# RWKV scan: order of PSUM banks for 64x64 products, and two 128-column steps turned into 64x64 products

## The chip, the cores and the metric

One core of one Trainium2 chip runs the whole program. The time is device microseconds of one execution, as the median of several runs; lower is better. All data are float32. TensorE is called PE below, VectorE DVE, ScalarE ACT, GpSimd POOL and SyncE SP.

## The reference, cut to what matters

The program is one step of a two-layer trunk: an attention and HGRN2 layer, an RWKV-7 layer, an MLP behind each. The change is in the RWKV-7 layer alone. Its mixer runs, for 16 heads of size 64, forward and backward over 512 sample tokens and 128 prompt tokens, this recurrence:

```
def step(s, inp):
    r_t, w_t, k_t, v_t, kk_t, a_t = inp
    sa = jnp.einsum('bhvk,bhk->bhv', s, -kk_t)
    s = s * w_t[:, :, None, :] + sa[..., None] * (kk_t * a_t)[:, :, None, :] + v_t[..., None] * k_t[:, :, None, :]
    return s, jnp.einsum('bhvk,bhk->bhv', s, r_t)
...
kk = kk * lax.rsqrt(jnp.maximum(jnp.sum(kk * kk, axis=-1, keepdims=True), 1e-24))
...
mu = jnp.mean(y, axis=-1, keepdims=True)
var = jnp.mean(jnp.square(y - mu), axis=-1, keepdims=True)
```

The sums over the 64 elements of a head (of kk squared, of y, of y centred and squared, and of the bonus r k) are the "head sums" below.

## The kernel before, in words

The kernel does the recurrence in chunks of 64 tokens. Inside a chunk the products of the states' updates are a triangular matrix that is inverted by repeated squaring; from chunk to chunk a 64x64 state is carried. The work is laid out in 40 iterations: 8 pairs of heads (q) by 5 tiles of 128 tokens (two chunks), each iteration for both heads of the pair and both directions. Each task of an iteration m is a set of 8, 16 or 24 small products; d is the direction, h the head, hh the chunk. HALF[0] and HALF[1] are the partitions 0 to 63 and 64 to 127. A product whose operands lie in HALF[a] and whose output lies in HALF[b] uses one quarter (a, b) of PE's array, called a tile of the array here; a product with 64 rows and 128 output columns uses a half of it, as does one of 128 rows and 64 columns. A float32 product makes two matmul records and two weight loads in the trace; a transpose makes one of each.

The order of the work on each engine is written out by hand: PE_ORDER, DVE_ORDER, ACT_ORDER and POOL_ORDER list the tasks of an iteration, and each engine goes through its list 46 times (n from -4 to 41), skipping what does not apply. Engines wait for each other by semaphores. PE's list is:

```
PE_ORDER = ("gate", "values", "k_sum", "mean", "B4", ("G", 2), ("s1", -1), ("final", -1), "B5", ("GR", 1), "x0", ("B1", 1), ("A1", 2), "u0",
            "a", "bonus", "state", "prompt", "s0", ("B2", 1), "w", ("A2", 2), "x1", ("B3", 1), ("BT", 1), "u1", ("A3", 2), ("var", 1))
```

(in the first iteration of a pair w stands behind x1 and BT behind A3). A number is how many iterations ahead the task works. What the names mean:

- G, A1, A2, A3 (gram, squares, fourths, eighths): 16, 16, 24 and 16 products of 64x64 on all four tiles, for the inverse.
- B1 (diagonal), B2 (off_diagonal, 16 products each on four tiles, into banks 2 and 3), then B3, B4, B5 (first_block, second_block, third_block): three times on_token, 8 products of 64x64 each. Their operands and outputs lie in the same half, so they use two of the four tiles, and all of them write bank 2, columns 0 to 255. B3 waits for ACT's copy of bank 2 (NT, line 2383). DVE adds each result to DD (block, line 2505).
- GR (read_keys, line 2198): 8 products with 64 rows, 128 output columns and 128 moving columns, into banks 6 and 7; DVE masks them into KB (line 2494, two instructions).
- BT (turn_keys, line 2238): 8 transposes of the same keys, 64 rows and 128 columns, into banks 6 and 7; ACT copies them out (line 2393).
- The walk over the two chunks of an iteration: x (x0, x1: 4 products; DVE adds XV, line 2515), u (4 products of the states with the queries into banks 4 and 5, 4 of TTs with XS; ACT copies out, line 2399), s (8 products with 128 rows and 64 columns; DVE updates the states, line 2526). ACT line 2408 copies y out.
- Work on the side that uses banks 6 and 7 as GR and BT do, each behind the other's copy-out (`before`, evacuated): the head sums (head_sums, line 2079) for k_sum, mean, var and bonus; lora (prompt, w, a; line 2087: four tiles, 128 or 512 moving columns), values (five transposes, line 2132), gate (wide), state, final.

Nearly all products are issued through the helper `mm` at line 178, so the trace gives that line to them; the transposes of BT (2238) and of values (2132) have their own. ACT copies bank 3 of B2 into XV at line 2387, right after NT at line 2383. In the last iterations products of the next stage (out1, 128x128) stand between the tasks of the list ("ahead").

Of the kernel before, what the change touches and what calls it, by code (L numbers as in the profile page):

```python
# [17 lines left out]
ALU = mybir.AluOpType  # L18
# [85 lines left out]
HN = T // 2  # L104
# [11 lines left out]
def program(nc, a, o):  # L116
    with ExitStack() as ctx:
# [1951 lines left out]
        def rwkv_pe(pe):  # L2069
# [6 lines left out]
            def head_sums(rhs):  # L2076

                for b, (t0, n) in enumerate(GROUPS):
                    for h, r in enumerate(HALF):
                        ins = mm(PS[r, 6 + b, 0:n], CON[r, C_BD64 + 64 * h:C_BD64 + 64 * h + 64], rhs[r, t0:t0 + n])  # L2080
                return ins
# [65 lines left out]
            def on_token(bank, lhsT, rhs):  # L2147

                for hh, h, d in ALL8:
                    c0 = 128 * h + 64 * hh  # L2150
                    ins = mm(PS[HALF[d], bank, c0:c0 + 64], lhsT[HALF[d], h, hh, :], rhs[HALF[d], h, hh, :])
                return ins
# [39 lines left out]
            def read_keys(m):  # L2192
                if before[0]:
                    evacuated(pe, before[0])
                before[0] = ("GR", m)
                pe.wait_ge(S("rwkv_staged"), m + 1)
                for hh, d, h, c in units_of(m):
                    ins = mm(PS[:, 6 + h, 256 * d + 128 * hh:256 * d + 128 * hh + 128], BKD[d][HALF[h], c, :], ARD[d][HALF[h], c, :])
                ins.then_inc(S("b_product"), 1)
# [21 lines left out]
            def first_block(m):  # L2221
                pe.wait_ge(S("b_scalar"), 4 * m + B_SC["N"])
                on_token(2, NT[:, :, 0], DD[:, :, 0]).then_inc(S("b_product"), 1)
# [9 lines left out]
            def turn_keys(m):  # L2233
                if before[0]:
                    evacuated(pe, before[0])
                before[0] = ("BT", m)
                for hh, d, h, c in units_of(m):
                    ins = nc.tensor.transpose(PS[:, 6 + h, 128 * d + 64 * hh:128 * d + 64 * hh + 64], BKD[d][HALF[h], c, :],
                                              CON[HALF[h], C_ID + 64 * h:C_ID + 64 * h + 64])
                ins.then_inc(S("b_product"), 1)  # L2240
# [23 lines left out]
            def walk_u(n, s):  # L2264
                q, k = n // 5, 2 * n + s
                pe.wait_ge(S("rwkv_x"), k + 1)
                for d, h, hh, c in each_dh(n, s):
                    mm(PS[HALF[h], 4 + d, 192 + 64 * hh:256 + 64 * hh], ST[d][HALF[h], c, :], ARD[d][HALF[h], place(q, c), 64:128],
                       start=False, stop=False, shared=True)
                for d, h, hh, c in each_dh(n, s):  # L2270
                    ins = mm(PS[HALF[d], 4 + h, 64:128], TTs[n % 2][HALF[d], h, 0, hh, :], XS[HALF[d], h, :], start=False, stop=True, shared=True)
                ins.then_inc(S("rwkv_u_psum"), 1)
# [24 lines left out]
        def rwkv_act(act, step):  # L2297
# [7 lines left out]
            def side(item):  # L2305
# [34 lines left out]
                elif kind == "bonus":  # L2340
                    act.wait_ge(S("rwkv_bonus_psum"), q + 1)
                    A.activation(BN[q % 2], pair(6), ACT.Copy, scale=64.0).then_inc(S("rwkv_bonus"), 1)
                elif kind == "var":
                    log_exp()
                    act.wait_ge(S("rwkv_var"), q + 1)
                    step(A.activation(RT2, pair(6), ACT.Ln, bias=EPSC[:, 1:2]))
# [82 lines left out]
        def rwkv_dve(dve, step):  # L2429
# [14 lines left out]
            def k_max(q):  # L2444
                dve.wait_ge(S("rwkv_k_sum"), q + 1)
                V.tensor_scalar(RT, pair(6), 1e-24 / 64, None, ALU.max).then_inc(S("rwkv_k_max"), 1)
# [56 lines left out]
            def block(m, what, out):  # L2503
                dve.wait_ge(S("b_product"), 8 * m + B_PR[what])
                V.tensor_tensor(out[:, :, 0], PS[:, 2, 0:256].rearrange("p (h c x) -> p h c x", h=2, c=2), DD[:, :, 0], ALU.add).then_inc(S("b_vector"), 1)  # L2505
# [24 lines left out]
            def side(item):  # L2530
# [3 lines left out]
                elif kind == "mean":  # L2534
                    dve.wait_ge(S("rwkv_mean"), q + 1)
                    V.tensor_tensor(K[:, q, :], YS, pair(6), ALU.subtract).then_inc(S("rwkv_centred"), 1)
# [480 lines left out]
```

## Time and profile before

| | |
|---|---|
| three runs | 2218.49, 2219.36, 2223.67 us; median 2219.36 us |
| span of the profiled execution (the only time known of it) | 2224.3 us |
| PE busy | 2055.9 us, 92% of the span, 26203 records |
| DVE, ACT, POOL busy | 64%, 47%, 14% |
| RWKV scan | about 1190 to 1725 us of the span |
| one pair of heads in the scan's steady part | 65 us (five iterations of 13.0 us) |

Busy time on PE is counted from a record's start to its modelled end. Records overlap, since a product of 64 columns takes 218 ns but starts a few ns behind its neighbour on another tile of the array; so the rows give starts and lengths of pieces, and the rate at which products go has to be taken from these.

### The profile page before, as it was taken

The page shows a single profiled execution, that of the slowest core. Times are in us where ns is not written, and L with a number is a line of the kernel's source. Part 1 is how long each engine was busy: PE and PEld are TensorE (multiplying, and loading weights), DVE is VectorE, ACT ScalarE, POOL GpSimd, SP SyncE. Part 2 cuts the span into 40 slices and gives each one's busy share as a digit, 9 for nine tenths or more (in the row PEclk, how much of TensorE's full clock was granted, in tenths as well). Part 3 has the DMA queues.
Part 4 walks back from the last instruction along what each step waited for, and adds up shares of the span by engine and source line. Part 5 has one row for each costly group of instructions (what it writes and reads, how often), then busy time and mean ns, then how long its engine had stood idle before and what let it go on. Part 6 is the DMA issues. An engine that isn't in the chain of part 4 may idle for free.

```text
span 2224.3 us, 60454 instructions
## 1 busy us (share of the span) xinstructions
PE 2055.9 (92%) x26203; PEld 1837.2 (83%) x26203; DVE 1414.5 (64%) x2698; ACT 1042.6 (47%) x1887; POOL 312.1 (14%) x542
## 2 busy tenths in 40 slices
PE   5999877898999999989997888898888989999999
PEld 2789754478999999957996777777777989999999
DVE  2242475655667675877535888887784468585857
ACT  5242363434535353565334665665654254434353
POOL 1000131101000000010002444444342200000000
PEclk8999999999999999999998999999999999999999
DMA  8212206960231322113210000000000221322212
GB/s 286 78 39 79 79 1 235 353 216 20 76 95 58 102 70 95 57 36 107 80 39 8 8 10 7 8 10 10 10 21 28 78 76 57 95 68 85 94 59 86
DMA packets 129764, 167.86 MB, mean 75 GB/s; under 512 B 13900, under 2 KB 87388, under 8 KB 129372
## 3 DMA queue, kind: packets, MB, share of 16 engines
q1 hardware_dynamic: 129500, 164.00, 22.0%
q8 instruction: 208, 3.41, 0.6%
q14 instruction: 56, 0.46, 0.1%
HBM read 160.44 MB, written 3.54 MB: 74 GB/s over the span
## 4 chain that ended last, share of the span: by engine, by line
PE 69%; DVE 14%; issue 7%; ACT 7%; POOL 1%; DMA 1%; PEld 1%; PEldq 0%; POOLq 0%; DVEq 0%; SPq 0%; ACTq 0%
PE psum L178 68%; DVE arena L2494 2%; ACT arena L1857 1%; ACT arena L1411 1%; DVE arena L2441 1%; DVE arena L2526 1%; DVE arena L2473 1%; DVE arena L2472 1%; PEld psum L178 1%; DVE arena L2465 1%; DVE arena L2505 1%; DVE small L1377 1%; DMA arena<-in_x_prompt 0%; DVE arena L2474 0%; PE psum L1342 0%
## 5 line engine op out<-in xcount | busy, mean ns | idle before, releaser
L178 PE MATMUL psum<-arena 64*64 64x64 f32 (+4 forms) x16064 | 582.3, 239 | 97.5 <-ACT arena L1411 14.9
L178 PEld LDWEIGHTS psum<-arena 64*64 64x64 f32 (+3 forms) x16064 | 462.5, 140 | 227.2 <-issue 109.4
L178 PE MATMUL psum<-hidden_high,weights_high 128*128 128x320 f32 x896 | 277.1, 309 | 0.5 <-DVE arena L1020 0.5
L178 PE MATMUL psum<-hidden_low,weights_high 128*128 128x320 f32 x896 | 276.9, 309 | 0.0
L178 PE MATMUL psum<-hidden_high,weights_low 128*128 128x320 f32 x896 | 276.9, 309 | 0.0
L178 PE MATMUL psum<-norm_high,weights_high 128*128 128x320 f32 x960 | 218.8, 309 | 0.0
L178 PE MATMUL psum<-norm_high,weights_low 128*128 128x320 f32 x960 | 218.7, 309 | 0.0
L178 PE MATMUL psum<-norm_low,weights_high 128*128 128x320 f32 x960 | 218.7, 309 | 0.0
L178 PEld LDWEIGHTS psum<-hidden_high,weights_high 128*128 128x128 f32 x896 | 168.2, 188 | 0.9 <-issue 0.7
L178 PEld LDWEIGHTS psum<-hidden_low,weights_high 128*128 128x128 f32 x896 | 168.2, 188 | 0.0
L178 PEld LDWEIGHTS psum<-hidden_high,weights_low 128*128 128x128 f32 x896 | 168.2, 188 | 0.0
L178 PEld LDWEIGHTS psum<-norm_low,weights_high 128*128 128x128 f32 x960 | 160.6, 188 | 0.0
L178 PEld LDWEIGHTS psum<-norm_high,weights_high 128*128 128x128 f32 x960 | 160.5, 188 | 0.0
L178 PEld LDWEIGHTS psum<-norm_high,weights_low 128*128 128x128 f32 x960 | 160.5, 188 | 0.0
L999 DVE TENSOR_TENSOR hidden<-hidden 128x640 f32<-128x640 f32 x32 | 26.4, 826 | 175.6 <-ACT hidden L946 175.6
L944 ACT ACTIVATE hidden<-psum 128x640 f32<-128x640 f32 x64 | 45.1, 705 | 189.4 <-PE psum L178 189.4
L899 ACT ACTIVATE weights_high<-weight_sums 128x512 fp32r<-128x512 f32 x128 | 76.8, 624 | 106.6 <-DVE weight_sums L918 55.7
L621 POOL TENSOR_TENSOR arena<-arena 128x640 f32<-128x640 f32 x24 | 41.7, 1739 | 570.7 <-ACT arena L613 569.9
L2610 POOL TENSOR_TENSOR arena<-arena,constants 64x128 f32<-64x128 f32 x160 | 79.1, 494 | 172.4 <-DVE arena L2485 157.8
L1020 DVE SCALAR_TENSOR_TENSOR arena<-psum,ada,arena 128x128 f32<-128x128 f32 (+2 forms) x208 | 83.7, 432 | 30.0 <-PE psum L178 29.1
L903 DVE TENSOR_TENSOR weights_low<-weight_sums,weights_high 128x512 fp32r<-128x512 f32 x128 | 88.5, 702 | 8.4 <-ACT weights_high L899 8.4
L899 ACT ACTIVATE weights_high<-weights 128x512 fp32r<-128x512 f32 x96 | 58.2, 622 | 68.2 <-PE psum L178 68.2
(268 smaller groups left out, 3985.6 us busy)
## 6 DMA issues: line engine op xcount, KB each, us to landing
weights<-in_mlp_w SPq DMA_DIRECT2D x64, 1024.0 KB, 5.4
arena<-in_ada_w SPq DMA_DIRECT2D x24, 2048.0 KB, 9.5
arena<-in_ab_w_in SPq DMA_DIRECT2D x6, 2048.0 KB, 7.9
arena<-in_ab_w_out SPq DMA_DIRECT2D x2, 2048.0 KB, 9.2
arena<-in_rwkv_wv SPq DMA_DIRECT2D x2, 2048.0 KB, 8.2
arena<-in_rwkv_wr SPq DMA_DIRECT2D x2, 2048.0 KB, 8.2
arena<-in_rwkv_wk SPq DMA_DIRECT2D x2, 2048.0 KB, 7.8
arena<-in_x_sample SPq DMA_DIRECT2D x1, 2048.0 KB, 10.0
```

The lines of the kernel that those rows point to most:

```text
L178: return nc.tensor.matmul(out, lhsT, rhs, start=start, stop=stop, skip_group_check=shared)
L621: G.tensor_tensor(total, a0 if k == 1 else total, (a0, a1)[k % 2], ALU.add).then_inc(S("norm_squares_added"), 1)
L899: A.activation(slots_of(WHI)[:, j], slot_raw(l, grp, i, j), ACT.Copy).then_inc(S("slot_high"), 1)
L903: V.tensor_tensor(slots_of(WLO)[:, j], slot_raw(l, grp, i, j), slots_of(WHI)[:, j], ALU.subtract)\
L944: A.activation(h, PS[:, 2 * j:2 * j + 2, 0:HN], ACT.Relu).then_inc(S("up_evacuated"), 1)
L999: V.tensor_tensor(h[:, H_T1:H_T3 + 1, :], h[:, H_B11:H_B22 + 1:3, :], h[:, H_B12:H_B12 + 1, :].broadcast_to([P, 2, HN]), ALU.subtract)\
L1020: ins = V.scalar_tensor_tensor(x, PS[:, bank, c:c + t1 - t0], gate[:, m, g:g + 1], x, ALU.mult, ALU.add)
L1377: step(V.tensor_reduce(st[:, 0:1], pair(2 * h, k), AXX, ALU.max))
L1411: A.activation(PR[m % 2][:, h, 0:k], pair(2 * h, k), ACT.Exp, scale=ATTN_SCALE, bias=st[:, 1:2], accum_out=st[:, 2:3]).then_inc(S("att_exp ...
L1857: A.activation(XI[s % 2][:, k, :], unit(U_H, 8)[:, k, :], ACT.Identity, scale=OMM[:, 8 * mrow + k:8 * mrow + k + 1])\
L2494: ins = V.tensor_tensor(KB[m % 2][:, h], PS[:, 6 + h, :].rearrange("p (d w x) -> p d w x", d=2, w=2), both.unsqueeze(2).broadcast_to([P, 2 ...
L2610: ins = G.tensor_tensor(P1[HALF[h], d, 0], QD[r, h, 0], units(r), ALU.add)
```

## The change

- on_token (B3, B4, B5): the order of the loops alternates the heads between the directions, and head h writes bank 2 + h, columns 256 to 383, in place of all in bank 2, columns 0 to 255. DVE's block reads from there. B3 waits for ACT's copy XV of bank 3 (line 2387) in place of NT of bank 2 (line 2383), because it now writes into bank 3.
- head_sums: two groups of 320 tokens in place of 512 and 128, in an order in which the halves write different banks. The four readers take two times 320 elements from two banks.
- read_keys (GR): 16 products of 64x64 with 128 moving columns, in place of 8 with 128 output columns.
- turn_keys (BT): 16 products of 64x64 with a 64x64 identity, in place of 8 transposes.
- walk_u (u): the same 8 products in another order, so that neighbours lie on different tiles of the array and in different banks.

```
             def head_sums(rhs):
 
-                for b, (t0, n) in enumerate(GROUPS):
-                    for h, r in enumerate(HALF):
-                        ins = mm(PS[r, 6 + b, 0:n], CON[r, C_BD64 + 64 * h:C_BD64 + 64 * h + 64], rhs[r, t0:t0 + n])
+                for h, g in ((0, 0), (1, 1), (0, 1), (1, 0)):
+                    r = HALF[h]
+                    ins = mm(PS[r, 6 + g, 0:HN], CON[r, C_BD64 + 64 * h:C_BD64 + 64 * h + 64], rhs[r, HN * g:HN * g + HN])
                 return ins
...
             def on_token(bank, lhsT, rhs):
 
-                for hh, h, d in ALL8:
-                    c0 = 128 * h + 64 * hh
-                    ins = mm(PS[HALF[d], bank, c0:c0 + 64], lhsT[HALF[d], h, hh, :], rhs[HALF[d], h, hh, :])
+                for h0 in range(2):
+                    for hh in range(2):
+                        for d in range(2):
+                            h = h0 ^ d
+                            c0 = 256 + 64 * hh
+                            ins = mm(PS[HALF[d], bank + h, c0:c0 + 64], lhsT[HALF[d], h, hh, :], rhs[HALF[d], h, hh, :])
                 return ins
...
                 for hh, d, h, c in units_of(m):
-                    ins = mm(PS[:, 6 + h, 256 * d + 128 * hh:256 * d + 128 * hh + 128], BKD[d][HALF[h], c, :], ARD[d][HALF[h], c, :])
+                    for r in HALF:
+                        ins = mm(PS[r, 6 + h, 256 * d + 128 * hh:256 * d + 128 * hh + 128], BKD[d][HALF[h], c, r], ARD[d][HALF[h], c, :])
                 ins.then_inc(S("b_product"), 1)
...
             def first_block(m):
-                pe.wait_ge(S("b_scalar"), 4 * m + B_SC["N"])
+                pe.wait_ge(S("b_scalar"), 4 * m + B_SC["XV"])
                 on_token(2, NT[:, :, 0], DD[:, :, 0]).then_inc(S("b_product"), 1)
...
                 for hh, d, h, c in units_of(m):
-                    ins = nc.tensor.transpose(PS[:, 6 + h, 128 * d + 64 * hh:128 * d + 64 * hh + 64], BKD[d][HALF[h], c, :],
-                                              CON[HALF[h], C_ID + 64 * h:C_ID + 64 * h + 64])
+                    for r in HALF:
+                        ins = mm(PS[r, 6 + h, 128 * d + 64 * hh:128 * d + 64 * hh + 64], BKD[d][HALF[h], c, r],
+                                 CON[HALF[h], C_ID + 64 * h:C_ID + 64 * h + 64])
                 ins.then_inc(S("b_product"), 1)
...
                 pe.wait_ge(S("rwkv_x"), k + 1)
-                for d, h, hh, c in each_dh(n, s):
+                at = {(d, h): (d, h, hh, c) for d, h, hh, c in each_dh(n, s)}
+                for d, h, hh, c in (at[0, 0], at[1, 1], at[1, 0], at[0, 1]):
                     mm(PS[HALF[h], 4 + d, 192 + 64 * hh:256 + 64 * hh], ST[d][HALF[h], c, :], ARD[d][HALF[h], place(q, c), 64:128],
                        start=False, stop=False, shared=True)
-                for d, h, hh, c in each_dh(n, s):
+                for d, h, hh, c in (at[0, 1], at[1, 0], at[0, 0], at[1, 1]):
                     ins = mm(PS[HALF[d], 4 + h, 64:128], TTs[n % 2][HALF[d], h, 0, hh, :], XS[HALF[d], h, :], start=False, stop=True, shared=True)
                 ins.then_inc(S("rwkv_u_psum"), 1)
...
-                    A.activation(BN[q % 2], pair(6), ACT.Copy, scale=64.0).then_inc(S("rwkv_bonus"), 1)
+                    A.activation(in_halves(BN[q % 2]), halves(6), ACT.Copy, scale=64.0).then_inc(S("rwkv_bonus"), 1)
...
-                    step(A.activation(RT2, pair(6), ACT.Ln, bias=EPSC[:, 1:2]))
+                    step(A.activation(in_halves(RT2), halves(6), ACT.Ln, bias=EPSC[:, 1:2]))
...
-                V.tensor_scalar(RT, pair(6), 1e-24 / 64, None, ALU.max).then_inc(S("rwkv_k_max"), 1)
+                V.tensor_scalar(in_halves(RT), halves(6), 1e-24 / 64, None, ALU.max).then_inc(S("rwkv_k_max"), 1)
...
-                V.tensor_tensor(out[:, :, 0], PS[:, 2, 0:256].rearrange("p (h c x) -> p h c x", h=2, c=2), DD[:, :, 0], ALU.add).then_inc(S("b_vector"), 1)
+                V.tensor_tensor(out[:, :, 0], PS[:, 2:4, 256:384].rearrange("p h (c x) -> p h c x", c=2), DD[:, :, 0], ALU.add).then_inc(S("b_vector"), 1)
...
-                    V.tensor_tensor(K[:, q, :], YS, pair(6), ALU.subtract).then_inc(S("rwkv_centred"), 1)
+                    V.tensor_tensor(in_halves(K[:, q, :]), in_halves(YS), halves(6), ALU.subtract).then_inc(S("rwkv_centred"), 1)
```

`halves(6)` is columns 0 to 319 of banks 6 and 7; `in_halves(x)` is x as two groups of 320.

## Rows read from the trace of the kernel before

**Rows 1.** The page's busy line: us, share of the span, records.

```profile
PE 2055.9 (92%) x26203; PEld 1837.2 (83%) x26203; DVE 1414.5 (64%) x2698; ACT 1042.6 (47%) x1887; POOL 312.1 (14%) x542
```

**Rows 2.** Busy us (records) in stretches, one pair of heads each; then clock, DMA.

```profile
1311.00:1376.00 65.00, 58.17 (x1893) 48.14 (x1894) 53.41 (x118) 39.88 (x96) 28.78 (x60) 1.00 0.04 9
```

**Rows 3.** Waits in the scan's steady part, 1220 to 1680: us, times, longest.

```profile
DVE arena L2515 <- PE psum L178: 27.1, 29, 2.2
...
PE psum L178 <- issue: 4.6, 8, 1.0
```

**Rows 4.** The chain that ended last, 1190 to 1735: start us, us, what.

```profile
1196.22 4.21 PE psum L178 x80
...
1255.75 0.39 PE psum L2238 x8
1256.15 1.12 PE psum L178 x43
...
1311.03 3.56 PE psum L178 x96
...
1698.21 5.22 PE psum L178 x100
...
1709.83 0.39 PE psum L2238 x8
...
1719.67 2.87 PE psum L178 x40
```

**Rows 5.** PE in order of time: B5's last records, then GR, then x0.

```profile
1312.79 0.40 PE L178 MATMUL psum<-arena 64*64 64x64 f32 x8
...
1313.12 1.16 PE L178 MATMUL psum<-arena 64*128 64x128 f32 x15
...
1314.21 0.34 PE L178 MATMUL psum<-arena 64*64 64x64 f32 x7
```

**Rows 6.** PE in order of time, pieces of one kind of product.

```profile
1310.28 0.68 PE L178 MATMUL psum<-arena 64*64 64x64 f32 x16 [0.37 <-DVE arena L2505]
...
1340.37 0.67 PE L178 MATMUL psum<-arena 64*64 64x128 f32 x16 [0.46 <-DVE arena L2494]
...
1366.61 0.73 PE L178 MATMUL psum<-arena 64*64 64x64 f32 x16
```

**Rows 7.** PE in order of time: B5 to u0 in one piece.

```profile
1312.55 3.43 PE L178 MATMUL psum<-arena 64*64 64x64 f32 x120
```

**Rows 8.** PE in order of time: x1 and B3, BT, u1 and A3.

```profile
1319.88 0.81 PE L178 MATMUL psum<-arena 64*64 64x64 f32 x24 [0.48 <-DVE arena L2526]
1320.62 0.46 PE L2238 MATMUL psum<-constants,arena 64*128 64x64 f32 x8
1321.01 1.20 PE L178 MATMUL psum<-arena 64*64 64x64 f32 x48
```

**Rows 9.** DVE in order of time, the XS add of x0 in two iterations.

```profile
1314.62 0.29 DVE L2515 TENSOR_TENSOR arena<-psum,arena 128x128 f32<-128x128 f32 x1 [0.89 <-PE psum L178]
...
1353.11 0.29 DVE L2515 TENSOR_TENSOR arena<-psum,arena 128x128 f32<-128x128 f32 x1
```

**Rows 10.** DVE in order of time: the add after A3.

```profile
1322.24 0.42 DVE L2500 TENSOR_TENSOR arena<-psum,constants 128x256 f32<-128x256 f32 x1 [1.09 <-PE psum L178]
```

**Rows 11.** Late in the scan: an x0 behind GR, ACT's XV copy, the next BT.

```profile
1641.90 0.52 PE L178 MATMUL psum<-arena 64*64 64x64 f32 x18 [0.21 <-ACT arena L2408]
...
1684.70 0.38 ACT L2387 ACTIVATE arena<-psum 128x256 f32<-128x256 f32 x1
...
1685.63 0.46 PE L2238 MATMUL psum<-constants,arena 64*128 64x64 f32 x8
```

**Rows 12.** First iteration of a pair, in order of time: head sum, B4, B4's reader.

```profile
1347.37 1.29 PE L178 MATMUL psum<-arena,constants 64*64 64x512 f32 x8 [0.69 <-ACT arena L2393]
1348.50 0.63 PE L178 MATMUL psum<-arena 64*64 64x64 f32 x16
...
1349.86 0.42 DVE L2505 TENSOR_TENSOR arena<-psum,arena 128x256 f32<-128x256 f32 x1
```

## The prediction

> **What bounds the kernel now.** I read the page first [rows 1]: PE is busy 92% of the span. The change touches only the RWKV scan, so I cut that out in stretches of one pair of heads [rows 2]: of 65 us PE is busy 58.2 and DVE 53.4, with a granted clock of 1.00, the 2.4 GHz level. Neither is alone the bound: DVE's XS add, the one after x, waits for PE 27.1 us in 460 [rows 3], and the chain below goes over both. Both go through fixed lists and hold each other up, so a saving on PE counts only where the chain that ended last runs over PE. So I took that chain piece by piece and held against it every GR, BT and u [rows 4]. On it lie 14 of the scan's 40 GR (the first in the piece at 1196.22, the last in that at 1698.21), 12 of 40 BT (1255.75 to 1709.83) and 23 of 80 u (the first in the piece at 1256.15, the last in that at 1719.67). In the steady part these are, of five iterations, one GR (n mod 5 = 3, the piece of 3.56 us at 1311.03), one BT in that same iteration and two or three u. The rest of the chain is DVE's and ACT's.
>
> **The change part by part.** A record's own length stands in every piece: 0.22 us for 64 moving columns, 0.27 for 128. The last record starts that much before the piece's end.
>
> *The rate of products.* B4, 16 records on two tiles of the array, takes 0.68 us (the row at 1310.28 in [rows 6]): 0.68 - 0.22 = 0.46 us from first start to last. x1 and B3 together, 24 records, take 0.81 [rows 8]: 0.59 from first to last. Both come out with a step of 0.058 us for each group (one record on each tile in use), 0.05 once where PE begins again, and up to 0.02 inside a group: 0.05 + 7 x 0.058 = 0.46, and 0.05 + 2 x 0.058 + 7 x 0.058 + 0.02 = 0.59. With 128 moving columns lora shows four tiles at once (1340.37 in [rows 6]): 16 records in 0.67, so (0.67 - 0.27 - 0.05 - 0.02) / 3 = 0.11 per group of four.
>
> *GR* [rows 5]. B5 ends at 1313.19, so its last record started at 1312.97, and GR starts at 1313.12: 0.15 where 0.058 is usual, 0.09 too much. GR itself is 1.16 - 0.27 = 0.89 from first to last start. The last starts at 1314.01, x0 at 1314.21: 0.20 where the step is 0.11, 0.09 too much; then 0.05 for beginning again. After the change there are 32 records in 8 groups of four, at lora's step 7 x 0.11 + 0.02 = 0.79 in place of 0.89, with no change of shape on either side. Saved: 0.09 + 0.10 + 0.09 + 0.05 = 0.33 us, and 0.02 for the stagger inside the last group, 0.35 at most; I take 0.34. The piece B5 to u0 checks it [rows 7]: 120 records, 3.43 - 0.22 = 3.21 from first to last. B5, x0, B1, A1 and u0 are 8 + 2 + 8 + 8 + 7 = 33 steps, 1.91; u0's own loss 0.05; that leaves 1.25 for GR with both changes of shape, less the 0.90 of its 8 steps: 0.35.
>
> *BT* [rows 8]. B3's last record starts at 1320.69 - 0.22 = 1320.47, BT at 1320.62 (0.15), its last 0.24 later, u1 another 0.15 later, and 0.05 for beginning again: 0.59. New: 8 groups of four at 0.058 = 0.47 in place of 0.24, and one step of 0.058 to follow: 0.53. Saved 0.06 where u1 follows at once. But its result comes later: 0.49 after B3's last start, not 0.39. ACT's copy of it and the next side task stand behind that. In the first iteration of a pair BT stands behind A3, with no array change to save in front of it that is not covered by a wait, and the next head sum waited 0.69 us for ACT's copy [rows 12]; there the head sum and B4 come up to 0.24 later. B4's reader on DVE starts at 1349.86, and B4's results were there at about 1348.50 + 0.63 = 1349.13. So 0.24 is covered by 0.7 us; without that cover it would cost 0.24 x 8 = 1.9 us.
>
> *u* (1366.61 in [rows 6]). The same 16 records on the same two tiles as B4, but 0.73 in place of 0.68: its second four go tile A, A, B, B. In the new order they alternate: saved 0.05.
>
> *Bank order of on_token and head_sums.* B4 writes all to one bank from two halves, and still goes at one pair per 0.058, the step at which four-tile work goes too; the two tiles are full. Value 0. From below: nothing to gain under the step of a full tile. From above: nothing, as x0 writes two banks at the same step. A head sum is 8 records in 1.29 us [rows 12], two halves side by side. Its stream per half is 640 columns twice, before and after; the sum over 512 and 128 is that over 320 and 320. Value 0, within 0.05 each way; the readers have the same 640 elements.
>
> *The Trainium skill speaks against splitting into more products.* Its page "TensorE: Matmul & The Clock Gate" (Part 1, the section on 56 against 53.3 ns) says starts are never closer than about 25 ns. By that figure BT's 32 records would last 0.8 us, an estimate, and 12 x 0.33 = 4 us of the gain would be gone. The trace says otherwise for just this kind of product on four tiles: B1 and A1, 64 records, fit into 3.21 us with all the rest only at 0.058 us for four, 15 ns each [rows 7], so the rule gets no chance here.
>
> *B3's new wait.* XV's copy ends 0.28 us after NT's. In most iterations x1's wait stands between. In the last of a pair it doesn't: late in the scan XV ends at 1684.70 + 0.38 = 1685.08 [rows 11], while B3, whose last record starts 0.15 before BT at 1685.63, began at 1685.02. B3 will be 0.06 late and a hop of some 0.05 more: 0.1 to 0.15. Behind it stand BT, u1 and A3. Three such lie on the chain (near 1461, 1592 and 1685): 3 x 0.15 = 0.45 us lost.
>
> *More instructions.* 16 records more for GR and 24 for BT, on 379 per iteration (1893 / 5): 11%. PE's idle time put to "issue" is 4.6 us, 8 times [rows 3]. If it grows with the count, 0.5 us, at most all on the chain; at least 0. I take 0.3.
>
> *Sum.* GR: twice in the last iterations (1640, 1679) x0 waited for ACT's y copy behind GR (1641.90 in [rows 11]), so half counts: 12 x 0.34 + 2 x 0.17 = 4.4. BT: 12 x 0.06 = 0.7. u: 23 x 0.05 = 1.15. Together 6.3; less 0.45 and 0.3: 5.5 us. This is also close to the most that can come of it, since the old chain stays a lower bound for the new time. Is there room beside it? At x0 of the steady part DVE sat idle 0.89 (1314.62 in [rows 9]), more than the 0.34; at A3, after BT and u1, 1.09 [rows 10], more than 0.11. Where GR isn't on the chain DVE comes to x0 straight from other work, with no idle time before it (1353.11 in [rows 9]), and nothing is won.
>
> The profiled execution has a span of 2224.3 us, 4.9 above the median and 0.6 above the slowest of the three runs. A difference of 5.5 us does not depend on that. Against the median 2219.4: **2213.9 us**, 0.25% faster. A measurement of this kernel can tell about 0.3% (6.7 us) from no change.
>
> **The rivals.**
>
> *A: the cover is thinner.* DVE, ACT and the walk are each busy or late right behind PE's chain; what PE gives, they take back. For it: DVE busy 53.4 of 65. Against it: the two idle times above. The tail's five GR have no such row, and if these 1.5 us, half of the u and the fill's three GR go, 5.5 - 1.5 - 0.6 - 1.0 = 2.4: 2217 us.
>
> *B: more than the chain shows.* PE's other GR, BT and u shorten too, 40 x (0.34 + 0.06) + 80 x 0.05 = 20 us in all. If the chain as inferred misses part of PE's share, say half of the rest, (20 - 6.3) / 2 = 7 more: 2207 us. For it: DVE waits for PE 27.1 us at x alone [rows 3]. Against: behind many of these waits ACT or DVE is next.
>
> *C: slower. Two products with the same rows and the same moving columns don't run side by side.* New GR and BT are all such pairs. Then GR goes at 0.11 per two records, 16 x 0.11 = 1.8 us, 0.9 more less 0.34 of saved changes; BT at 0.058 per two, 0.93, 0.46 more less 0.06. On the chain: 14 x 0.56 + 12 x 0.40 = 12.6, less 1.15 of u, plus 0.75: 12 us slower, 2231.6. It decides from a group step in GR of 0.15 up (0.04 x 8 x 14 = 4.5 us, the gain gone). Against it: lora's two column halves share rows and moving columns, and go at 0.11 per four.
>
> *D: BT's later result stalls the side tasks.* The 1.9 us above and as much again where ACT's copy stands before its u copy: gain 5.5 - 3.8 = 1.7, 2217.7. I count it with A.
>
> **How the numbers follow.** Forecast 0.58, A with D 0.22, B 0.14, C 0.06. The forecast's own range is 2212 to 2216 (terms of 0 to 0.6 each way, and 1 us for the medians). For 8 in 10 it reaches over all of A to 2218 and into B to 2209. Faster by over 0.3% needs 2212.7 or less: 0.35 of the forecast (0.20), B whole (0.14): 0.34. Slower: C, 0.05. Same: the rest, 0.61.
>
> **What would show it.** In the trace after: B5, GR, x0 and B1 in one piece without a change of shape, B5 to u0 in 3.04 us in place of 3.43 [rows 7]; BT a part of a 64x64 piece, B3 to A3 0.1 shorter where nothing waits; u alone 0.68. The step from 1311 to 1376 would be 64.4 to 64.6 us in place of 65, the rest of the gain in fill and tail. DVE's idle time before x0's add would fall from 0.89 to 0.55 at n mod 5 = 3 and nothing move in the other four. B4 and the head sums as long as before. The prediction is wrong if GR's 32 records take over 0.95 us from first to last, if the step per pair of heads falls by over 1 us, or if it doesn't fall.

## The result, and the profile after: slower, and PE runs out of instructions

| | before | after |
|---|---|---|
| median of 20 runs each, on the same chips | 2223.5 us (2218.5 to 2230.0) | 2229.8 us (2225.6 to 2238.2) |
| span of the profiled execution | 2224.3 us | 2225.5 us |
| ratio | 1 | 1.0031, 95% interval 1.0024 to 1.0039 |

The change costs 0.31%, 6.9 us, where 5.5 us of gain were forecast. The two profiled executions differ by only 1.2 us in their spans, though the scan alone is 9.4 us longer (the table below): before the scan the changed kernel's execution happens to be 9 us ahead. Most of that, 6.7 us by the 3700th matmul record (518.4 us before, 511.6 after, where the 1500th came at 280.3 and 279.5), arises in stages that the change doesn't touch. So the scan is compared below, and not the spans.

The page of the changed kernel has, below its head, PE's line: against [rows 1] PE is busy 6.1 us *less*, with 1600 matmul records and 1600 weight loads more (3200 / 40 = 80 PE instructions more per iteration).

```profile
span 2225.5 us, 63654 instructions
...
PE 2049.8 (92%) x27803; PEld 1839.1 (83%) x27803; DVE 1413.0 (63%) x2698; ACT 1041.5 (47%) x1887; POOL 311.8 (14%) x542
```

So the array was busy for less time. The local sums of the prediction can be read in PE's order of time in the changed kernel. First B5 to u0 [rows 7], then B3's end and BT (the piece of 27 records, with no change of shape on either side) and u1 and the first product of A3 behind it [rows 8], then a u that stands alone [rows 6]:

```profile
1437.76 3.19 PE L178 MATMUL psum<-arena 64*64 64x64 f32 x136
...
1324.57 0.68 PE L178 MATMUL psum<-constants,arena 64*64 64x64 f32 x27
1325.06 1.29 PE L178 MATMUL psum<-arena 64*64 64x64 f32 x48
...
1360.36 0.68 PE L178 MATMUL psum<-arena 64*64 64x64 f32 x16 [0.38 <-DVE arena L2521]
```

B5 to u0 went from 3.43 to 3.19 us (3.04 was forecast), u from 0.73 to 0.68, and u1 starts 0.03 us after BT's last record (1324.57 + 0.68 - 0.22 = 1325.03) and not 0.15. Of the 0.15 us missing in GR, the records' starts show where it is: B5's last starts at 1438.17 and GR's first at 1438.30, as late as when the shape changed there, and its second group comes 0.16 us later where I had 0.11; the other six steps are 0.11, and x0 follows 0.09 behind the last.

What cost the time is in PE's waits over the scan, 1195 to 1720 (engine, line, what it waited for: us in total, times, longest):

```profile
PE psum L178 <- issue: 18.6, 37, 2.0
PE psum L178 <- ACT arena L2405: 8.1, 17, 0.7
...
PE psum L178 <- DVE arena L2521: 5.5, 13, 0.8
...
DVE arena L2521 <- PE psum L178: 35.9, 38, 2.1
```

In [rows 3] "issue" was 4.6 us, 8 times, and it is no more than that in the kernel before over this wider stretch. It is now 18.6 us, 37 times, and the longest wait of PE; 21 of the 37 are of 0.3 us or more and make 15.4 of the 18.6 us. "Issue" says that nothing in the records released the instruction. DVE's XS add (L2515 before, L2521 now) waits for PE hardly longer than it did; over the same stretch 1195 to 1720 it was, in the kernel before:

```profile
DVE arena L2515 <- PE psum L178: 34.7, 38, 2.2
```

Here is one of PE's stops for "issue", PE in order of time:

```profile
1387.03 0.68 PE L178 MATMUL psum<-arena 128*64 128x64 f32 x15
1388.06 2.27 PE L178 MATMUL psum<-arena 128*64 128x64 f32 x102 [0.35 <-issue]
1390.12 0.27 PE L178 MATMUL psum<-constants,arena 64*64 64x64 f32 x1
...
1390.22 0.52 PE L178 MATMUL psum<-constants,arena 64*64 64x64 f32 x20
1392.17 0.39 PE L178 MATMUL psum<-constants,arena 64*64 64x64 f32 x10 [1.43 <-issue]
```

BT stops in its middle for 1.43 us, after 22 of its 32 records and at the end of a run of 127 records without a pause (the chain below has 125 of them). No operand can be missing there: it is one task with one wait ahead of it. And the stop lies on the chain that ended last:

```profile
1387.70 0.35 issue
1388.06 2.68 PE psum L178 x125
1390.74 1.43 issue
1392.17 1.86 PE psum L178 x58
```

The DMA view shows a queue of its own for instructions, q8, in packets of 16 KB. In the stretch from 1264 to 1272, where no other queue is at work, two of them can be seen in 40 slices of 0.2 us, at 1264.9 and 1268.9:

```profile
GB/s 0 0 0 0 82 0 0 0 0 0 0 0 0 0 0 0 0 0 0 0 0 0 0 0 82 0 0 0 0 0 0 0 0 0 0 0 0 0 0 0
...
q8 instruction: 2, 0.03, 1.8%
```

PE stops and goes on at 1267.70 and 1271.37, 2.8 and 2.4 us behind their starts:

```profile
1267.70 1.12 PE L178 MATMUL psum<-arena 64*64 64x64 f32 x31 [0.73 <-issue]
...
1271.37 2.63 PE L178 MATMUL psum<-arena 64*64 64x64 f32 x80 [0.33 <-issue]
```

The stop in BT ends 2.3 us after the start of the packet of 1389.88. So it is throughout: of the changed kernel's 21 stops of 0.3 us and more, 20 end 2.2 to 2.8 us after a 16 KB packet of q8 has started (the other, the longest, 3.0 us), and so do all five of the kernel before. Between two packets there are never less than 3.3 us, in either kernel; the median is 4.16 us before and 3.86 after. Over the stretch 1200 to 1700, first before, then after:

```profile
q8 instruction: 115, 1.88, 1.6%
```

```profile
q8 instruction: 124, 2.03, 1.7%
```

Where the stops fall in the list of work says the same, more sharply. Here are the three stretches between the four stops that end at 1388.06, 1392.17, 1399.69 and 1403.9 (records of PE and of PEld):

```profile
1388.06:1392.16 4.10, 2.68 (x127) 2.39 (x128) 2.74 (x9) 2.41 (x7) 1.04 (x2) 1.00 0.20 52
1392.17:1399.68 7.51, 6.94 (x253) 6.07 (x252) 5.61 (x13) 3.98 (x9) 2.75 (x7) 1.00 0.02 4
1399.69:1403.89 4.20, 3.22 (x127) 2.78 (x127) 0.87 (x3) 3.61 (x11) 1.53 (x4) 1.00 0.01 4
```

That is 255, 505 and 254 instructions: one, two and one times the contents of a packet, as worked out below. Of the 20 distances between neighbouring long stops of the changed kernel 18 are whole multiples of 252 to 256; the two others are those on either side of the stop at 1549.29. PE stops where one packet's instructions are used up, whatever task it is in. Where two stops stand one packet apart, as here, that packet's worth takes 3.5 to 4.2 us.

The Trainium skill ("Runtime: NRT & Kernel Launch", Instruction fetch mechanics) says that an engine's instructions come in blocks of 16 KiB, 256 instructions, from a DMA queue. The counts agree: 16022 matmul records and 16019 weight loads (their row stands under "Instructions alone" below) in 127 packets are 252 per packet. The same section of the Trainium skill says that the fetch is hidden because instructions are dispatched more slowly than blocks come in. That does not hold here. By this trace's numbers alone, 252 per 3.3 us is 76 per us at the very most, and 252 per 3.5 to 4.2 us is 60 to 72 per us where PE starves; the scan asks for 32041 / 518.9 = 62 per us in the mean, and for about 117 per us in BT (27 records and as many loads in 0.68 - 0.22 = 0.46 us, the row at 1324.57).

### The profile page after: what moved, and what is told of

Same layout as the page of the kernel before. It is cut to its first block, busy times and chain, and to the rows that moved or that the text cites. A ratio compares the mean times of both kernels' runs of the same rounds, so it can differ in the third digit from the quotient of the medians.

```text
span 2225.5 us, 63654 instructions
## 1 busy us (share of the span) xinstructions
PE 2049.8 (92%) x27803; PEld 1839.1 (83%) x27803; DVE 1413.0 (63%) x2698; ACT 1041.5 (47%) x1887; POOL 311.8 (14%) x542
## 4 chain that ended last, share of the span: by engine, by line
PE 71%; DVE 10%; issue 7%; ACT 7%; POOL 2%; DMA 1%; PEld 1%; PEldq 0%; POOLq 0%; DVEq 0%; SPq 0%; ACTq 0%
PE psum L178 70%; DVE arena L2500 1%; ACT arena L1857 1%; ACT arena L1411 1%; DVE arena L2471 1%; PEld psum L178 1%; DVE small L1377 1%; DMA arena<-in_x_prompt 0%; DVE arena L2447 0%; PE psum L1342 0%; DVE arena L2479 0%; ACT arena L642 0%; DVE arena L2478 0%; DVE arena L2532 0%; POOL arena L621 0%
## 5 line engine op out<-in xcount | busy, mean ns | idle before, releaser
L178 PE MATMUL psum<-arena 64*64 64x64 f32 (+5 forms) x16704 | 578.0, 241 | 104.3 <-ACT arena L1411 15.0
L899 ACT ACTIVATE weights_high<-weights 128x512 fp32r<-128x512 f32 x96 | 58.2, 622 | 68.3 <-PE psum L178 68.3
```

Source lines behind the costliest of these rows:

```text
L178: return nc.tensor.matmul(out, lhsT, rhs, start=start, stop=stop, skip_group_check=shared)
L899: A.activation(slots_of(WHI)[:, j], slot_raw(l, grp, i, j), ACT.Copy).then_inc(S("slot_high"), 1)
```

## The experiments

Theory S: PE runs out of instructions, since the change adds 80 per iteration and each stretch of small products on four tiles eats them faster than they are fetched. Theory L: BT's longer stream and later result hold up what stands behind. Theory B: the bank order, the head sums' groups or B3's new wait do it.

All kernels beside the one before; "scan" is from the first product of the walk's state updates to the last, "stops" is PE's idle time in it put to issue, both read from one profiled execution, and the packets are those of 1200 to 1700. The ratios are to the runs of the kernel before on the same chip. Two ratios differ for sure only where they are some 0.0015 apart. The profiled execution of e4_gr_bt_alone was its slowest, that of e3_old_gr its fastest.

| kernel | PE instr. per iteration | ratio, 95% | scan us | stops us (times) | packets |
|---|---|---|---|---|---|
| before | 0 | 1 | 509.4 | 4.6 (8) | 115 |
| e1_old_gr_bt | 0 | 0.9992, 0.9981 to 1.0003 | 509.4 | 5.7 (13) | 114 |
| e8_gr_and_u | +32 | 0.9993, 0.9984 to 1.0001 | 508.2 | 7.1 (18) | 119 |
| e2_old_bt | +32 | 0.9989, 0.9980 to 0.9998 | 507.0 | 6.5 (20) | 120 |
| e3_old_gr | +48 | 1.0045, 1.0032 to 1.0058 | 518.5 | 13.5 (21) | 119 |
| e4_gr_bt_alone | +80 | 1.0028, 1.0016 to 1.0040 | 514.7 | 14.5 (24) | 124 |
| e12_change_again | +80 | 1.0035, 1.0022 to 1.0048 | 517.5 | 15.4 (30) | 125 |
| e5_half_bt | +48 | 1.0017, 1.0008 to 1.0025 | 515.6 | 14.0 (30) | 120 |
| e6_half_both | +16 | 1.0003, 0.9993 to 1.0014 | 510.7 | 8.5 (18) | 116 |
| e7_late_bt | +36 | 1.0014, 1.0006 to 1.0023 | 516.1 | 9.5 (21) | 118 |
| e9_before_fewer | -112 | 0.9968, 0.9956 to 0.9981 | 503.6 | 1.0 (2) | 98 |
| e11_old_bt_fewer | -80 | 0.9955, 0.9941 to 0.9969 | 502.4 | 1.9 (7) | 103 |
| e10_after_fewer | -32 | 0.9975, 0.9965 to 0.9986 | 505.2 | 4.1 (10) | 110 |
| e13_before_padded | +80 | 1.0043, 1.0031 to 1.0056 | 521.8 | 11.8 (20) | 123 |
| e14_fewer_padded | -32 | 0.9976, 0.9963 to 0.9988 | 506.1 | 1.5 (2) | 109 |

### Which part does it

The changed kernel with GR, BT or both as before, and the kernel before with the new GR and BT alone:

```
 def turn_keys(m):                                   # e1, e2
-        for r in HALF:
-            ins = mm(PS[r, 6 + h, ...], BKD[d][HALF[h], c, r], CON[HALF[h], C_ID + 64 * h:...])
+        ins = nc.tensor.transpose(PS[:, 6 + h, ...], BKD[d][HALF[h], c, :], CON[HALF[h], C_ID + 64 * h:...])
 def read_keys(m):                                   # e1, e3
-        for r in HALF:
-            ins = mm(PS[r, 6 + h, ...], BKD[d][HALF[h], c, r], ARD[d][HALF[h], c, :])
+        ins = mm(PS[:, 6 + h, ...], BKD[d][HALF[h], c, :], ARD[d][HALF[h], c, :])
```

> The changed kernel with both GR and BT as before; the order of u, the banks of on_token and head_sums and B3's new wait stay. PE has the instruction count of the kernel before. Theory S (supply: PE runs out of instructions, because GR and BT as 64x64 products add 80 instructions per iteration): PE's idle time put to issue in the scan falls back from 18.6 us (37 times) to about 5 (8), and the time is 0 to 2 us under that of before. Rival W (wait and banks: B3's wait for XV, or the new banks and groups, cost the time): still 4 to 8 us slower than before. Rival R (GR's and BT's own records last longer than computed): as S in the time, but the issue idle time does not tell it apart; the next runs do.

> The changed kernel with BT as transposes as before; GR is 64x64. 32 instructions per iteration more than before. Theory S: issue idle 8 to 12 us, time within 3 us of before, since what GR saves by the two changes of shape (0.34 us on 14 of the chain) stands against part of the stalls. Rival W: as the changed kernel, 6 us slower. Rival R for BT: all of the loss is gone, 4 to 5 us faster than before.

> The changed kernel with GR as before; BT is 64x64. 48 instructions per iteration more than before. Theory S: issue idle 8 to 14 us, 3 to 7 us slower than before, since BT saves only 0.06 us on the chain at a time. Rival W: 6 to 10 us slower. Rival R for GR: 1 to 2 us faster.

> The kernel before with GR and BT as 64x64 products and nothing else of the change. 80 instructions per iteration more. Theory S: issue idle 15 to 20 us, 5 to 9 us slower than before, like the changed kernel plus what u's order gave. Rival W: 4 to 5 us faster than before.

Measured: 0.9992, 0.9989, 1.0045, 1.0028. With both as before the loss is gone; bank order, head sums, u and B3's wait together are worth nothing or 0.1%: theory B falls. The new BT does it. With it the kernel is slow whether GR is new (the change) or old; without it, new GR and all, it is at least as fast as before. PE's waits in the scan of e2_old_bt, the idle time that was 18.6 us:

```profile
PE psum L178 <- issue: 6.5, 20, 0.8
```

The sizes were less well forecast than the signs: by theory S e2_old_bt would have had 8 to 12 us of stops (6.5 measured), e4_gr_bt_alone 15 to 20 (14.5), and e3_old_gr would have been 3 to 7 us slower (10). e2_old_bt and e3_old_gr ask for the same mean number of instructions per us (30172 / 507.0 and 30827 / 518.5, both 59.5), with 6.5 and 13.5 us of stops: the mean alone doesn't set them, the place where the instructions are added counts too.

The change was also run once more, unaltered, with the other kernels on one chip; it came out as the first time, with 15.4 us of stops:

> The changed kernel again, beside these on the same chip, for a second profile. All theories: 5 to 8 us slower than before. Theory S: issue idle in the scan 12 to 22 us, but at other places than in the first profile, since the fetches' landings vary.

The last of this group has GR and u new, and banks, head sums and BT's transposes as before, on the kernel before:

```
# before, with the change's read_keys and walk_u; on_token, head_sums, their readers and turn_keys as before
```

> The kernel before with GR as 64x64 products and the new order of u, nothing else: no new banks, no new wait for XV, no new groups of the head sums. Theory S: as the changed kernel with BT as transposes or better by the 0.5 us that B3's wait was computed at: 2 to 4 us faster than before, issue idle 5 to 9 us. If the banks matter (they let neighbours write side by side), it is slower than that kernel by over 2 us.

0.9993 beside the 0.9989 of e2_old_bt: the bank order and B3's wait are nothing that can be told.

### Number of instructions, or BT's place and length?

Half of the new BT, and half of BT and GR, in the same places with steps of the same length:

```
-                    for r in HALF:
+                    for r in HALF[0:1]:            # e5: in turn_keys; e6: in read_keys too
```

> The changed kernel, with BT made of only the 8 products whose output lies in partitions 0 to 63 (the other half of the turned keys is left out, and the copy-out multiplies by zero). These 8 go one behind the other on two tiles, so BT's stream lasts as long as that of the 16 on four tiles (8 steps of 0.058 us), without a change of shape, and its result comes as late; but 32 instructions per iteration are gone. Theory S (supply of instructions): most of BT's loss goes: issue idle in the scan from 18.6 us to 6 to 10, and the time 0 to 4 us under that of before. Rival L (BT's stream is longer and its result later, 0.1 to 0.2 us, and that costs the time): no change against the changed kernel, 5 to 7 us slower than before.

> As the run with half of BT, and GR too is made of only its 8 products for partitions 0 to 63 (the masks are zero, so the masked keys are). GR's stream stays 8 steps of 0.11 us. Against the changed kernel 64 instructions per iteration are gone; against the kernel before there are 16 more. Theory S: issue idle 4 to 7 us and 3 to 6 us faster than before, the gain that was predicted for the chain. Rival L: as the changed kernel, 5 to 7 us slower than before.

1.0017 and 1.0003: less with each step, as theory S has it, and BT's stream is as long as in the change. But neither theory's numbers were met: e5_half_bt is 3.8 us slower than before (theory S: 0 to 4 faster; theory L: 5 to 7 slower), e6_half_both 0.7 slower (theory S: 3 to 6 faster), and in e5_half_bt the stops had hardly fallen (14.0 us), with 32 instructions fewer. So I made BT late with few instructions, by a 64x128 product between its transposes:

```
                 for hh, d, h, c in units_of(m):
+                    if (hh, d, h) == (1, 1, 0):
+                        mm(PS[:, 7, 256:384], BKD[d][HALF[1], c, :], ARD[d][HALF[1], c, :])
                     ins = nc.tensor.transpose(...)
```

> The changed kernel with BT as transposes, and one product more in it (64 rows, 128 output and 128 moving columns, into unused columns of bank 7) before the last two transposes: BT's stream and its result are some 0.2 us later at a price of 4 instructions. Theory S: within 3 us of the same kernel without that product, which was 2.5 us faster than before; where BT is on the chain 12 x 0.2 = 2.4 us are lost, so 1 to 3 us faster to 1 slower than before. Rival L: 8 to 12 us slower than that kernel, 6 to 10 slower than before.

1.0014, 3.1 us slower than before and 0.25% above e2_old_bt: a longer BT costs as well. Theory S had it at most 1 us slower than before, theory L 6 to 10 us slower; neither was met, and the stops rose too (9.5 us for 6.5). But the product makes the whole stream 0.28 us longer, u1 and A3 start that much later, and five iterations take 65.5 us where e2_old_bt takes 64.65. In the change BT with u1 is *shorter*: the row at 1325.06 above. The run shows what PE time at BT is worth, and not what a late copy is worth.

The next three take supply out of the question from the other side. Half of the products of G, A1 and A2 are left out, those of two of the four tiles:

```
             def from_keys(m, c0, lhsT, rhs):
                 for hh, d, h, c in units_of(m):
+                    if d != h:
+                        continue
...
-                to_home(0, 0, QD[:, :, 1], QD[:, :, 0])
+                to_home(0, 0, QD[:, :, 1], QD[:, :, 0], TWO)     # and the four others of squares and fourths
```

> The kernel before with 112 instructions per iteration fewer, at the same stream length: gram, squares and fourths leave out the products on two of their four tiles (masks and the copies behind them are zero, to keep numbers small). What is left of each task goes in as many steps of 0.058 us as before. It is the reference for the two runs beside it. Theory S (supply): it is 2 to 5 us faster than before, issue idle in the scan 0 to 2 us in place of 4.6, and the scan's blocks of five iterations are even at 64.9 us. Rival L (only lengths and order matter): as before, within 1 us.

> The changed kernel with the same 112 instructions per iteration fewer; it has 32 fewer than the kernel before. Theory S: all the loss is gone: issue idle 0 to 4 us, time within 2 us of the kernel before with fewer instructions, so 2 to 6 us faster than before; its blocks are 64.6 to 64.9 us. Rival L (BT's longer stream): 5 to 7 us slower than the kernel before with fewer instructions.

> The changed kernel with BT as transposes, and the same 112 instructions per iteration fewer. Theory S, with the predicted gain of GR and u on the chain (4.4 + 1.15, less 0.45 for B3's wait): 5 us faster than the kernel before with fewer instructions, blocks 64.6 us, issue idle 0 to 2 us. If GR's gain was computed too high, 1 to 3 us faster. The difference to the changed kernel with fewer instructions is what BT costs by itself: -0.7 us by the sum, some +1 us if its later result counts.

The array's steps stay as long as they were. Five iterations of e9_before_fewer, against [rows 2], have 281 records fewer and PE is busy for 58.0 us and not 58.2:

```profile
1272.00:1337.00 65.00, 58.00 (x1612) 47.99 (x1612) 53.36 (x118) 40.11 (x98) 29.00 (x60) 1.00 0.04 9
```

Still the kernel before gains 0.32% from it, and the changed one gains 0.56% (1.0031 to 0.9975). So the change costs 0.31% with the full number of instructions, and 0.07% (1.5 us) where there is more room: at least 5 of its 7 us are supply. And with BT's transposes the same base is 0.13% (2.9 us) *faster* than e9: there the forecast gain of GR and u is seen, somewhat over half of its 5.1 us. What the new BT costs over the old with this room, 0.20% (4.4 us), is for the most part not its late result either, as far as one profile of each can show. The runs of e10 and e11 go side by side up to iteration 14 and lose 1.1 us by iteration 15 and 1.9 us in iteration 35; in iteration 35 the chain of e10_after_fewer has, between the same records,

```profile
1657.83 0.41 issue
...
1662.22 1.05 issue
```

where e11_old_bt_fewer has 0.17 us, and in iteration 15 it has one of 0.82 us. So instructions run short there even with 32 fewer than in the kernel before. In undisturbed iterations the two are the same: 64.43 and 64.50 us for five.

### Instructions alone

All these took something away. The last two add just the number of instructions that the change adds, 80 per iteration, with GR, BT and u untouched: products on the two tiles that B3, B4 and B5 leave idle, into columns that nobody reads. They lie in bank 3, so B3 waits for XV, as in the change.

```
             def on_token(bank, lhsT, rhs, padded=(0, 1)):
                 for hh, h, d in ALL8:
                     c0 = 128 * h + 64 * hh
+                    if d == 0 and hh in padded:
+                        for e in range(2):
+                            mm(PS[HALF[1 - e], bank + 1, 256 + c0:256 + c0 + 64], lhsT[HALF[e], h, hh, :], rhs[HALF[e], h, hh, :])
...
-                pe.wait_ge(S("b_scalar"), 4 * m + B_SC["N"])
+                pe.wait_ge(S("b_scalar"), 4 * m + B_SC["XV"])
```

> The kernel before, with GR, BT and u untouched, but with extra products whose results nobody reads: in B3, B4 (8 each) and B5 (4), on the two tiles of the array that these steps leave idle, into unused columns of bank 3. That is 20 products, 80 PE instructions per iteration, the same number that the change adds. The step of 0.058 us per group stays, so the pieces should keep their length but for 0.02 us in the last group of each; B3 waits for XV as in the changed kernel. Theory S (PE runs out of instructions): idle time of PE put to issue rises from 4.6 us to 12 to 20 us in the scan, and the time by 7 to 14 us less nothing, ratio 1.003 to 1.006. Theory L (what cost the time is BT's longer stream and later result): both are as before here, so issue idle stays at about 5 us and the ratio is 1.000 to 1.0008 (three times 0.15 us at B3 and 0.02 us at each block).

> The kernel with 112 PE instructions per iteration less (half of the products of gram, squares and fourths left out, as in the run before_fewer), and with the 80 extra instructions per iteration of the padded kernel: 32 fewer than the kernel before. Theory S: what counts is the number per iteration and not which products they are: about as before or a little faster, issue idle 2 to 5 us, ratio 0.997 to 1.000. If the extra products cost by themselves, whatever the supply, it would stand as far above before_fewer (0.9968) as the padded kernel stands above before; under theory S that distance is less than half of it.

The kernel before, so padded, takes 1.0043, as much as the change or more, and stops for want of instructions 20 times. With the 112 instructions left out the same padding costs 0.08% (0.9968 to 0.9976). So of its 0.43%, 0.35% is the number of instructions by itself: 7.8 us for 80 per iteration. The scan of the padded kernel (from:to and length, then busy us and records of PE, PEld, DVE, ACT and POOL, granted clock), and PE's waits in it, at two lines here:

```profile
1208.04:1729.80 521.76, 459.81 (x16039) 382.26 (x16036) 399.10 (x882) 300.08 (x724) 216.19 (x455) 1.00 0.05 12
...
PE psum L178 <- issue: 9.0, 18, 1.0
...
PE psum L2241 <- issue: 2.8, 2, 1.6
```

and of the one with fewer:

```profile
1207.54:1713.61 506.07, 452.23 (x13944) 376.80 (x13940) 398.64 (x882) 300.16 (x724) 217.82 (x455) 1.00 0.05 12
...
PE psum L177 <- issue: 1.5, 2, 0.8
```

The number of instructions and the ratio of e14_fewer_padded are those of e10_after_fewer (both 32 below the kernel before; 0.9976 and 0.9975), though the products added are others. Theory S's ratios for both runs were met; the stops were just under its numbers, 11.8 us for 12 to 20 and 1.5 for 2 to 5. Theory L had the padded kernel at 1.0008 at most. Not all of a shortage seems to show as idle time: the padded kernel's PE is also busy for 8.0 us more than before, of which 3.8 are the padding's own (452.2 against the 448.5 of e9_before_fewer).

The same row of the kernel before, of e9_before_fewer and of the changed kernel, for the sums above (from:to and length, then busy time and records of PE, PEld, DVE, ACT and POOL; the records of PE and PEld together are PE's instructions):

```profile
1212.86:1722.29 509.43, 451.79 (x14479) 376.04 (x14476) 399.32 (x882) 299.95 (x724) 215.67 (x455) 1.00 0.05 12
```

```profile
1207.35:1710.94 503.59, 448.47 (x12383) 372.76 (x12380) 398.49 (x882) 299.80 (x724) 216.95 (x455) 1.00 0.05 12
```

```profile
1203.97:1722.82 518.85, 450.98 (x16022) 379.88 (x16019) 398.86 (x882) 298.80 (x724) 215.51 (x456) 0.99 0.05 12
```

## Why the prediction was wrong

- *"More instructions", 0.3 us, at most 0.5*: this term failed. It is the largest part of the miss: with 7.8 us in its place the sum comes out 2 us slower than before. I let the 4.6 us of issue idle grow with the count, by 11%. They grew fourfold, to 18.6. By the runs the term is at least 5.3 us in the change (0.31% less 0.07%) and 7.8 us for the same number added by itself. The row I took it from was right, but growth in proportion to the count was wrong: those 8 stops were a buffer running empty near its limit (57 per us asked for in the mean before and 62 after, 60 to 72 per us delivered where PE starves), and such stops grow far faster than the count as the demand comes near the limit. The shortest distance between packets and the count of q8 would have shown it in the trace of before: 115 packets in 500 us are one per 4.35 us, where two never stand closer than 3.3, and dense stretches between them.
- *GR, 0.34 us each*: the mechanism held (no change of shape, four tiles, steps of 0.11), the size did not. B5 to x0 is 1.05 us in place of 1.24, so 0.19 each. The late first product of GR was no matter of shape, and its second group is late by 0.05 more.
- *BT, 0.06 each*: held as a length on the array. B3's last record to u1's last is 0.95 us in place of 1.05, of which 0.05 is u's.
- *u, 0.05*: held, 0.68 for 0.73. *Bank order and head sums, 0*: held (e8_gr_and_u against e2_old_bt, 0.9993 and 0.9989). *B3's wait*: inside that difference.
- *The sum without the instruction term*, 5.8 us, or 5.1 without BT's 0.7: of the 5.1 us 2.9 were measured where supply has room (e11_old_bt_fewer against e9_before_fewer), and 2.4 without (e2_old_bt). With 0.19 for GR's 0.34 on 13 of them 2.0 of the 2.2 us missing are accounted for.
- *The whole miss*, from 5.5 us faster to 6.9 slower, is 12.4 us. In differences between runs: 5.0 for the instruction term (5.3 in place of 0.3), 2.2 for GR, u and B3's wait as above, and 5.1 for BT, which cost 4.4 us in e10_after_fewer over e11_old_bt_fewer where 0.7 of gain stood. Of these 4.4 us 3.0 come in the two iterations with stops, so they belong to the instructions as well. For the rest no row shows a cause.
- *The step of 64.4 to 64.6 us per pair of heads*: it is there where no stop falls in it, 64.43 in e10_after_fewer, 64.65 in e2_old_bt, 64.89 at best in the change (64.93 before). In the change most pairs have such stops: 65.4, 66.6, 64.9, 67.6, 65.4 and 70.6 us for the second to the seventh, where the kernel before has 64.9, 64.9, 65.0, 65.7, 66.0 and 66.6.
- *Rival C*, the one that ended slower, was not it: the pairs with the same rows run side by side at 0.058 and 0.11 us. *Rival D* (BT's later result, 3.8 us): in undisturbed iterations nothing of it is seen; late in the scan it can't be told from the stops. I had the right row in hand and no rival for it.

What stays open: where exactly a stop falls depends on where the packets fall in the list of work. Why 32 instructions more in GR cost nothing (e2_old_bt, e8_gr_and_u) and 48 in BT cost 0.4% or more (e3_old_gr) is in keeping with BT standing behind x1 and B3 in the thickest stretch of small products, where its 64 instructions go in about 0.6 us (1324.41 to 1325.04); this was not tried by moving BT. Why e5_half_bt and e7_late_bt came out between the theories stays open as well, and so do the 16 short stops, 3.2 us together. Of the kernels that leave nothing out e2_old_bt is the fastest, 0.11% faster than before (0.02% to 0.20%).

## What to carry to other kernels

A change that makes PE's array faster with more, smaller instructions has a second price: what the instruction fetch can bring. Before it, count PE's instructions per us in the stage, matmul records and weight loads together, set them against the densest spacing of the instruction queue's packets in the trace, and take any idle time put to "issue" in the middle of a task as the sign that the limit is near (here their distances were whole packets' worths of instructions, which settles it); from there, price added instructions by a run in which just their number is added. Of two changes with the same gain on the array take the one with fewer instructions: here the new GR alone was free, the new BT was not.

## What the runs showed of the hardware

- PE takes instructions from a DMA queue of its own, in packets of 16 KB (252 instructions each by the counts of this trace). Two packets never started less than 3.24 us apart in any kernel run here (e6_half_both; 3.31 in the two kernels of the change), although one packet is in flight for only 1.0 to 1.2 us (medians of the runs): at most 78 instructions per us (252 / 3.24). Over twelve packets in a row the mean was never under 3.71 us (e12_change_again), 68 per us.
- A stop for want of instructions ends mostly 2.2 to 2.8 us after a packet's start (139 of the 162 stops of 0.3 us and more in all kernels run here), in the changed kernel 1.25 to 1.6 us after the packet is in. Such stops stand whole multiples of 252 to 256 instructions apart. One can split a task in two, and the trace puts it to "issue".
- At a mean of 57 instructions per us (28955 / 509.4, before) the stops are 4.6 us of the scan, at 62 they are 18.6, at 49 (24763 / 503.6, e9_before_fewer) 1.0. At 59.5 they were 6.5 us in one kernel and 13.5 in another, so the place of the instructions counts too.
- Four products of 64x64 on four tiles go at 0.058 us together, 15 ns each, also where two of them share rows and moving columns.
